# Seven half-size products in all four FFN passes, with new homes for the weights

## What is computed

```python
def reference(x, c, ada_w, ada_b, norm_mix_g, norm_ffn_g, ...):
    for layer in range(DEPTH):
        sh1, sc1, g1, sh2, sc2, g2 = ada_modulation(c, ada_w[layer], ada_b[layer])
        h = rmsnorm(x, norm_mix_g[layer]) * (1.0 + sc1) + sh1
        if layer % 2 == 0:
            y = ...          # short convolution and gated linear recurrence, then w_out0
        else:
            z = jax.nn.gelu(jnp.einsum('bsd,de->bse', h, w_in1[j]) + b_in1[j])
            y = spatial_gating_mixer(z, gm_ln_g[j], gm_ln_b[j], gm_ws[j], gm_bs[j])
            y = jnp.einsum('bse,ed->bsd', y, w_out1[j])
        x = x + g1 * y
        h = rmsnorm(x, norm_ffn_g[layer]) * (1.0 + sc2) + sh2
        hid = jnp.square(jax.nn.relu(jnp.einsum('bsd,df->bsf', h, w_ff1[layer])))
        x = x + g2 * jnp.einsum('bsf,fd->bsd', hid, w_ff2[layer])
    return rmsnorm(x, final_g)
```

## Time and profile before

| | us |
|---|---|
| median of 3 executions | 2680.87 |
| lowest | 2675.13 |
| profiled execution, its own time | 2678.5 |
| its span in the profile (core 4, the slowest) | 2676.9 |
| the fastest core in it | 2652.6 |

### The profile page before, as it was taken

One profiled execution on the slowest core, in us unless ns is written; L12 is line 12 of the kernel. 1 busy time (PEld: TensorE's weight loads), 2 busy tenths in 40 slices (PEclk: granted clock), 3 DMA queues, 4 the chain that ended last, 5 costly groups with the idle time before them and its releaser, 6 DMA issues.

```text
span 2676.9 us, 52954 instructions; the slowest of 8 cores (2652.6 to 2676.9 us)
## 1 busy us (share of the span) xinstructions
PE 2553.7 (95%) x18009; PEld 1685.3 (63%) x18204; DVE 1866.4 (70%) x3387; ACT 1468.8 (55%) x2467; POOL 863.4 (32%) x956
## 2 busy tenths in 40 slices
PE   3999999999899999999999999998999999999998
PEld 1444444445566676788888444443766676788887
DVE  3577777777555566888877667676655666787887
ACT  4787777784545552443434665644545553545544
POOL 4456555442433440000002354513433440112111
PEclk9999999999999999999999999998999999999999
DMA  9744444448356338865647666654244336232331
GB/s 192 149 137 111 111 111 111 111 95 189 87 128 159 108 103 161 175 137 124 150 109 162 172 191 172 163 141 127 80 138 146 95 108 148 100 120 80 127 112 64
DMA packets 126426, 348.34 MB, mean 130 GB/s; under 512 B 13904, under 2 KB 16464, under 8 KB 115280
## 3 DMA queue, kind: packets, MB, share of 16 engines
q1 hardware_dynamic: 106464, 265.77, 32.8%
q0 software_dynamic: 19152, 78.65, 17.9%
q10 hardware_dynamic: 544, 0.52, 0.1%
HBM read 301.90 MB, written 117.44 MB: 157 GB/s over the span
## 4 chain that ended last, share of the span: by engine, by line
PE 77%; DMA 9%; issue 4%; ACT 4%; POOL 3%; DVE 3%; SPq 0%; another core or an unknown queue 0%; DVEq 0%; ACTq 0%; POOLq 0%
PE ps L750 23%; PE ps L1371 14%; PE ps L1328 13%; PE ps L1233 11%; PE ps L1638 4%; DMA xs<-sb_arena 3%; DMA sb_arena<-xs 3%; PE ps L1018 3%; PE ps L1584 3%; PE ps L1193 2%; PE ps L991 2%; POOL sb_arena L699 1%; DMA sb_arena<-w_in 1%; ACT L412 1%; DMA sb_arena<-x 1%
## 5 line engine op out<-in xcount | busy, mean ns | idle before, releaser
L750 PE MATMUL ps<-sb_arena 128*128 128x512 bf16 x3973 | 907.6, 380 | 13.6 <-DMA sb_arena<-w_in 6.6
L750 PEld LDWEIGHTS ps<-sb_arena 128*128 128x128 bf16 x4096 | 395.8, 98 | 462.8 <-issue 13.1
L699 POOL TENSOR_TENSOR sb_arena<-sb_arena 128x512 f32<-128x512 f32 (+1 forms) x259 | 359.1, 1387 | 783.7 <-ACT sb_arena L696 757.9
L1328 PE MATMUL ps<-sb_arena 128*128 128x256 bf16 x3584 | 404.4, 274 | 16.6 <-DVE sb_arena L1213 10.0
L1371 PE MATMUL ps<-sb_arena 128*128 128x256 bf16 x3584 | 398.6, 273 | 4.8 <-DVE sb_arena L1378 4.8
L1328 PEld LDWEIGHTS ps<-sb_arena 128*128 128x128 bf16 x3584 | 352.1, 98 | 64.6 <-issue 14.0
L1371 PEld LDWEIGHTS ps<-sb_arena 128*128 128x128 bf16 x3584 | 350.2, 98 | 46.9 <-issue 5.8
L1233 PE MATMUL ps<-sb_arena 128*128 128x256 bf16 x3136 | 351.9, 273 | 5.0 <-DVE sb_arena L1248 4.8
L1207 ACT ACTIVATE sb_arena<-ps 128x512 f32<-128x512 f32 x288 | 169.7, 592 | 298.1 <-PE ps L750 219.9
L1233 PEld LDWEIGHTS ps<-sb_arena 128*128 128x128 bf16 x3136 | 304.7, 98 | 44.0 <-issue 8.5
L1340 DVE SCALAR_TENSOR_TENSOR sb_arena<-ps,sb_arena 128x256 f32<-128x256 f32 x640 | 261.2, 475 | 96.0 <-PE ps L1328 95.0
(11 more groups left out here) (150 smaller groups left out, 3061.3 us busy)
## 6 DMA issues: line engine op xcount, KB each, us to landing
xs<-sb_arena SPq DMA_DIRECT2D x320, 256.0 KB, 4.5
sb_arena<-xs SPq DMA_DIRECT2D x160, 512.0 KB, 6.5
sb_arena<-w_ff POOLq DMA_DIRECT2D x32, 1024.0 KB, 13.0
sb_arena<-ada_w POOLq DMA_DIRECT2D x72, 256.0 KB, 5.6
sb_arena<-x SPq DMA_DIRECT2D x64, 256.0 KB, 3.8
hs<-sb_arena SPq DMA_DIRECT2D x16, 1024.0 KB, 10.9
sb_arena<-hs SPq DMA_DIRECT2D x16, 1024.0 KB, 5.8
sb_arena<-xs SPq DMA_DIRECT2D x64, 256.0 KB, 4.4
```

The costliest lines, as they stand in the source:

```text
L699: G.add(adds, lambda e, c=c, to=to: e.tensor_tensor(out=to, in0=dst, in1=tmp[:, c % 2, :], op=ALU.add), [b_dst, tmpb[c % 2]], [b_to], key, ...
L750: parts = [(lambda e, kc=kc: e.matmul(bk(B), w[:, kc, col0:col0 + 128], hT[:, kc, :], start=kc == 0, stop=kc == 7), [wb, hb[kc]], c_mm(512 ...
L1328: parts.append((lambda e, m=m, fc=fc, h=h, r=r: e.matmul(bk(Bm)[:, h * H:(h + 1) * H], w[:, fc, m * 128:(m + 1) * 128], r, start=h == 0 an ...
```

## The change

All passes now use `ff1_halves` from tile 1 on and `ff2` for the second product; tile 0 of each pass takes the plain first product, and `first_sums` runs in each of them. Pass 0 now makes the five input sums of each tile as well (`input_sums`): four go to other buffers or are made first, the fifth in place in `hT`. `hT` is one buffer instead of two in turn, and hs is stored in two halves, since the in-place sum must follow the store of its half. The sums need homes: FFS is dealt anew, the w_ff1 chunks of pass 1 take the very homes of those of pass 0, and home 15 holds the temporaries in all passes. The modulation vectors leave (0,0): 32 of 48 are made in (0,1), five a tile, and 16 in m1, three a tile. In the last tile of m1 every second one of the eight multiplies goes to VectorE.

```diff
@@ -1022,12 +1022,13 @@
-TP = (52.5, 49.0)
-
-FFS = {(0, 0): ((5, 4, 3, 6), (1, 2, 0, 9), (10, 11, 7)),
-       (0, 1): ((12, 13, 14, 15), (10, 11, 7, 9), (1, 2, 0), (5, 4, 3), 6),
-       (1, 0): ((0, 1, 2, 7), (9, 6, 12, 13), (14, 15, 10)),
-       (1, 1): ((3, 4, 5, 11), (14, 15, 10, 13), (9, 6, 12), (0, 1, 2), 7)}
+TP = 49.0
+
+FFS = {(0, 0): ((5, 4, 3, 6), (1, 2, 0, 9), (10, 11, 7), (12, 13, 14)),
+       (0, 1): ((5, 4, 3, 6), (12, 13, 14, 10), (11, 7, 1), (2, 0, 9)),
+       (1, 0): ((12, 13, 14, 10), (7, 1, 5, 4), (3, 6, 0), (2, 9, 11)),
+       (1, 1): ((12, 13, 14, 10), (2, 9, 11, 3), (6, 0, 7), (1, 5, 4))}
+FTMP = 15
@@ -1043,25 +1044,20 @@
-    hT0b[:] = tile(Region([(A_HT, A_HT + 8192)]), "hT0", [128, 8, TT], BF16, nbuf=8)[1]
-    o["hT"] = [(hT0, hT0b), tile(Region([(8 * SLOT, 9 * SLOT)]), "fhT1", [128, 8, TT], BF16, nbuf=8)]
+    o["hT"] = tile(Region([(A_HT, A_HT + 8192)]), "hTh", [128, 8, TT], BF16, nbuf=16)
+    reg = Region([(FTMP * SLOT, FTMP * SLOT + SLOT)])
+    o["Th"] = {i: tile(reg, "Th%d" % i, [128, 4, H], BF16) for i in (1, 6, 7)}
+    reg = Region([(FTMP * SLOT + 6144, FTMP * SLOT + SLOT), (8 * SLOT, 9 * SLOT)])
+    o["part"] = [tile(reg, "part%d" % i, [128, 2, H], F32, nbuf=2) for i in range(3)]
+    o["z"] = tile(reg, "z", [128, 2, TT], F32, nbuf=2)
+    o["Td"] = tile(Region([(A_NRM + 8192, A_NRM + 10240)]), "Td", [128, 4, H], BF16)
...
@@ -1143,27 +1139,17 @@
-            dma("sp", lambda e: e.dma_start(out=hT, in_=hs_d[l][ti]), [hsb[l][ti]], hb, key + 10, d_hld[ti % 2],
+            dma("sp", lambda e: e.dma_start(out=hT, in_=hs_d[l][ti]), hsb[l][ti], hb, key + 10, d_hld[ti % 2],
-                [tmpb[c % 2], modbuf(l, 3, c), s1b[q]], [hb[c]], k, c_act(TT, False, 2))
-        dma("sp", lambda e: e.dma_start(out=hs_d[l][ti], in_=hT), hb, [hsb[l][ti]], key + 40, d_hst[ti % 2],
-            1024 * 1024)
+                [tmpb[c % 2], modbuf(l, 3, c), s1b[q]], hb[2 * c:2 * c + 2], k, c_act(TT, False, 2))
+        for i in range(2):
+            dma("sp", lambda e, i=i: e.dma_start(out=hs_d[l][ti, :, 4 * i:4 * i + 4], in_=hT[:, 4 * i:4 * i + 4, :]),
+                hb[8 * i:8 * i + 8], [hsb[l][ti][i]], key + 36 + 4 * i, d_hst[2 * (ti % 2) + i], 512 * 1024)
+        if ti:
+            input_sums(ti, key + 38)
...
+    def input_sums(ti, key):
+        Th = o["Th"]
+        for n, (dst, x, y, op) in enumerate((((None, o["Td"])[1 - p], (1, 0), (0, 0), ALU.subtract),
+                                             (Th[1], (0, 0), (1, 1), ALU.add), (Th[6], (0, 0), (0, 1), ALU.add),
+                                             (Th[7], (1, 0), (1, 1), ALU.add),
+                                             (None, (0, 1), (1, 1), ALU.subtract))):
+            if p:
+                dst, x, y, op = ((Th[1], (0, 0), (1, 1), ALU.add), (Th[6], (0, 0), (0, 1), ALU.add),
+                                 (Th[7], (1, 0), (1, 1), ALU.add), (None, (0, 1), (1, 1), ALU.subtract),
+                                 (None, (1, 0), (0, 0), ALU.subtract))[n]
+            xa, xbufs = hq(*x)
+            ya, ybufs = hq(*y)
+            da, dbufs = (dst[0], [dst[1]]) if dst else (xa, xbufs)
+            dve(lambda e, xa=xa, ya=ya, da=da, op=op: e.tensor_tensor(out=da, in0=xa, in1=ya, op=op),
+                xbufs + ybufs, dbufs, key + 0.1 * n, 0.6 if p else 0.8)
...
@@ -1224,9 +1226,11 @@
-            if i not in Th:
+            if i == 4 and not p:
+                r, rb = o["Td"][0], [o["Td"][1]] * 4
+            elif i not in Th:
                 kh, nh = {2: (0, 0), 5: (1, 1), 3: (0, 1), 4: (1, 0)}[i]
-                r, rb = hq(ti, kh, nh)
+                r, rb = hq(kh, nh)
             else:
                 r, rb = Th[i][0], [Th[i][1]] * 4
@@ -1278,7 +1282,7 @@
-            if m in FUSED:
+            if m in ((0, 3) if p else (0, 3, 6)):
@@ -1486,17 +1490,17 @@
-        b = base + TP[p] * ti + (4.0 if p and ti else 0.0)
+        b = base + TP * ti + (4.0 if ti else 0.0)
         if ti == 0:
             prepare(0, b - 50)
-        (ff1_halves if p and ti else ff1)(ti, b)
-        if p and ti == 0:
-            firsts = first_sums(l, w1, base)
+        (ff1_halves if ti else ff1)(ti, b)
+        if ti == 0:
+            firsts = first_sums(l, p, w1, base)
         if ti + 1 < ntiles:
-            prepare(ti + 1, b + TP[p] - 46 if ti or p or l else b + TP[p] - 40, stored.get(ti - 1, ()))
+            prepare(ti + 1, b + TP - 46 if ti or p or l else b + TP - 40, stored.get(ti - 1, ()))
         if after_tile:
             after_tile(ti, b, begun)
-        (ff2 if p else ff2_plain)(ti, b)
+        ff2(ti, b)
@@ -1567,9 +1571,9 @@
-    for n, (i, home) in enumerate(((2, 12), (3, 13), (0, 14), (1, 15))):
+    for n, (i, home) in enumerate(((2, 5), (3, 4), (0, 3), (1, 6))):
...
@@ -1628,9 +1632,10 @@
-            pool(lambda e, ec=ec, q=q: e.tensor_tensor(out=ymix[:, ec, :], in0=t1[:, q, :], in1=uT[:, ec, :],
-                                                       op=ALU.mult), [t1b[q], ub[ec]], [ymb[ec]], k,
-                 c_pool2(512))
+            two = ti + 1 == ntiles and ec % 2
+            G.add("dve" if two else "pool", lambda e, ec=ec, q=q: e.tensor_tensor(
+                out=ymix[:, ec, :], in0=t1[:, q, :], in1=uT[:, ec, :], op=ALU.mult), [t1b[q], ub[ec]], [ymb[ec]],
+                  k, c_dve(512) if two else c_pool2(512))
@@ -1654,62 +1660,58 @@
-        hooks = [hook(0, 2, 16), hook(1, max(5, -(-32 // ntiles)), 48)]
-    begun = phase_ffn(l, 0, base, o, w1, W, hooks[0])
-    g1 = [(base + NF - 150 + n, [begun[min(2 + n, ntiles - 1)]]) for n in range(4)]
-    g2 = [(base + NF - 24 + n, ()) for n in range(4)]
-    base += NF
-    w1, A = ffn_weights(l, 1, base, g1, g2)
-    half_buffers(l, o)
...
+    w1, A = ffn_weights(l, 1, base, [(base - 30 + n, ()) for n in range(4)], [(base - 24 + n, ()) for n in range(4)])
     W = ffn_sums(l, 1, A, base + 2)
-    begun = phase_ffn(l, 1, base, o, w1, W, hooks[1])
+    begun = phase_ffn(l, 1, base, o, w1, W, None if l else lambda ti, b, begun: vectors(
+        ti, max(5, -(-32 // ntiles)), 32, b + 8, 6.0, [begun[ti]]))
...
-        marks = phase_m1(base, spatial)
+        fr, frb = tile(Region([(SLOT, 2 * SLOT)]), "adaring4", [128, 4, D], BF16, nbuf=4)
+        ring = [(fr[:, i, :], frb[i], dsem()) for i in range(4)]
+        marks = phase_m1(base, spatial, lambda ti, b, marks: vectors(
+            ti, max(3, -(-16 // ntiles)), 48, b + 30, 3.0, [marks[ti]]))
```

129 lines of the change are left out of this document (53 added, 76 removed).

## The result

The changed kernel is slower by 1.4%: the ratio of its time to the kernel before is 1.0141, with a 95% interval of 1.0092 to 1.0190. The profiled execution takes 2717.2 us (span 2715.7 on core 6) against 2678.5 (2676.9), 38.8 of span more. Some executions ran longer at a lower granted clock (up to 3003.76 before, 2988.51 after) and take no part in any ratio, and where an experiment has no ratio (e_split, e_splitlast, e_sumslate, e_both, e_best2), its times are those of a core, or for e_splitlast of a stretch, at the usual clock.

A forecast was written before the change was run, and what follows sets the result against it. TensorE, busy 2553.7 of 2676.9 us, was taken as the bound. The terms -22.2 - 34.3 - 6.6 + 3.4 + 7 + 4.9 (small waits) sum to -47.8, from 2678.5 to 2631; range 2608 to 2662.

The forecast's parts named there:

- terms 1 and 2: First products of both passes 0, tiles 1 to 7: 224 half-width matmuls replace 128; layer 1 -22.2 us, layer 0 -34.3.
- term 2: Layer 0's pass 0, last seven tiles: 381.5 us falls toward 343.9, 3.3 kept back for the clock; -34.3 us.
- Does the new tile keep its 49.1?: New tile of passes 0: VectorE at 39 to 41 us, norm chain and hs store fit closely within 49.1.
- Rival (b): New tile of the first passes is paced by the hs store or norm chain at 51.5 us; 2659, chance 0.16.
- Rival (c): Weight loads at the two transitions come 13 us apart, +84 instead of +7, 2708; decides from 10.6; chance 0.06.
- Transitions (term 5): Last tile of each pass 0 into pass 1: late weight loads make TensorE wait; +7 us for both (+1 to +42).
- m1 (term 3): Between the FFNs: shared last multiplies -3.5 us, later norm matmul removing most of a wait -3.1; -6.6 (0 to -12).
- The -3.5 for the tail: m1's last tile: four of GpSimd's eight multiplies go to VectorE, 8.9 us instead of 12.4.
- "nothing" for the vectors: Sixteen modulation vectors of layer 1 moved to m1, three a tile, were to cost nothing, VectorE being less loaded there.
- Term 4: Layer 0's pass 0, tile 0 to 1: five input sums of 0.68 us on the chain; +3.4 us (0 to +8).

The follow-up runs named there:

- e_split: Changed kernel with every second of GpSimd's eight norm multiplies (tiles 1 to 7, passes 0) on VectorE; layer 1's pass 0 stretch took 362.9 us.
- e_splitlast: Changed kernel with four norm multiplies each on GpSimd and VectorE, SBUF adds onto X placed last, in passes 0; layer 1's pass 0 stretch took 370.6 us.
- e_sumslate: Changed kernel with each pass 1's weight sums held back until its first product has begun; second transition took 54.6 us on core 3.
- e_both: Changed kernel with norm multiplies shared four each, SBUF adds onto X placed last and pass 1's weight sums held back; span 2696.9 us.
- e_best2: Changed kernel with layer 1's pass 0 multiplies shared with VectorE, weight sums held back, m1's modulation vectors from its tile 2 on; span 2701.3 us.
- b_ff2: Kernel before with only the second product of passes 0 changed to the seven-product form; ratio 1.0115 to the kernel before.
- e_novec: Changed kernel without the 16 modulation vectors of m1, copies of others standing in; m1 took 427.7 us, ratio 1.0148 to the kernel before.
- e_dvemul: Changed kernel with all eight norm multiplies of tiles 1 to 7 of passes 0 on VectorE instead of GpSimd; ratio 1.0091 to the kernel before.

## Why the prediction was wrong

The forecast was 2631, 47.8 us less; the profiled execution took 2717.2, 38.7 more. The time lies outside the range, on the other side. By its steps:

- **Matmuls (terms 1 and 2).** The price of a matmul was right: without the multiplies seven tiles take 349.9, 50.0 each, with TensorE busy for 347.4 of them. The rule of the Trainium skill on the issue gap ("TensorE: Matmul & The Clock Gate", Back-to-back issue gap) does not hold here, as the rows of before said: by it the new form would cost more than the plain one, and these seven tiles are 16.2 under the 366.1 of before. In term 2 the room for a gain was read on the core with the longest (0,0); the median core had 8.6 us less of it.
- **"Does the new tile keep its 49.1?" failed**, and it carries the miss: in (1,0) a tile takes 53.7 to 55.2. I compared VectorE's busy time of 39 to 41 with the tile of 49.1 and found room. It became 42.9 (my higher figure with all 26 instructions stretched was 45.7), so the sum was not far off. But two things were left out. First, the sum of 39 to 41 has the stretching only on the bf16 sums that the trace of before showed stretched (L1311), not on the eight adds with both inputs in SBUF, which pass 0 did not have and which pass 1 runs with GpSimd mostly idle. These adds take 894 ns beside the multiplies, 476 to 479 without, and 476 with one input in PSUM. The Trainium skill ("SBUF — State Buffer", SBUF: two separate sides) says that VectorE with two SBUF inputs and a GpSimd instruction that reads SBUF exclude each other for a whole instruction; these numbers agree with it. I quoted the rule and used it as a sum over the tile. Second, the stretch falls within the 11.4 us of the multiplies, in which VectorE has no pause over 0.15 us and TensorE needs its results; that a mean over the tile has room says nothing there. The wait of 2.7 then costs another 1.4 to 1.7 through the clock in six of the seven tiles (6.76 to 7.07 against 5.40).
- **Where the change touches it.** I costed the second product of pass 0 at nothing, since both forms have 224 matmuls. b_ff2 shows that this swap alone costs 1.15% in the kernel before.
- **Rival (b)** had the right place (the new tile of the passes 0 is longer) with the wrong cause and price: 51.5 by the norm chain or the store. The store of hs now lands in 3.4 us (median of halves), and nobody waits for it. **Rival (c)** put its turning point at a spacing of 10.6; by its own sum the whole gain is gone only at 10.9. This changes nothing else.
- **Transitions (term 5).** The loads came as far apart as estimated: in (1,0) the first of the eight landed at 2272.7 and the last at 2324.3, 7.4 us apart. But besides the loads VectorE's list puts sums that wait for weights ahead of the last adds onto X. +7 became about +19 on the slowest cores with what follows in tile 0.
- **m1 (term 3).** The -3.5 for the tail was 0, since VectorE had other multiplies to run between its share; the waits on L699 stayed (3.7); and "nothing" for the vectors was about 5: their loads go with m1's first X and weights, which I had not looked at. The transfers of X there took a median of 19.8 us, and 13.7 in e_novec.
- **Term 4** was too small. From the first matmul of tile 0's second product tile 1 starts after 35.4 us instead of 31.0, and its first product then takes 33.5 instead of 27.9, where 24.6 were expected: TensorE waits for the normed input (L1165, 2.7 in three waits) and for the input sums (0.8), and the granted clock of this stretch is 0.85. So the first period of (0,0) is 68.9 against 58.9. Without the multiplies it is 62.7.

What stays open: why the normed input of tile 1 comes so late in (0,0), and what would help that pass. Behind its first period the split only trades the waits on the adds for waits on the input sums, and no variant that computes everything brought it under the 378.3 of the median core before.

## What to carry to other kernels

Before a helper engine is counted as room, look whether its instructions and VectorE's both take two operands from SBUF, and in which microseconds they meet; the adds with one operand in PSUM kept their 476 ns here. An engine with 20% of idle time can still hold up TensorE where it has to deliver before a PSUM bank is used again; read that stretch, not the tile. When a form of a computation is exchanged for another of equal matmuls, price its other engines' instructions. And before a stretch of the slowest core is taken as the base of a gain, look at the other cores: here its (0,0) was the longest of eight.

## What the runs showed of the hardware

One add of 128x256 in f32 with both inputs in SBUF took from 0.48 to 1.55 us beside GpSimd's multiplies of 128x512, and these were slower too (a mean of 1432 ns instead of 1272). After a wait of TensorE of 2.45 to 2.73 us the granted clock was 0.75 to 0.79 over the next 48 matmuls in six of seven cases and 1.00 in one; after waits of 2.46 in b_ff2 80 matmuls took 8.89 us at 1.00 in five tiles and 10.56 at 0.84 in two; the one of 1.75 looked at in e_dvemul left it at 1.00.
